# Expert stage of a two-layer trunk: permuted normed rows, picks dealt over the experts, modulation columns kept, gated rows dealt p-major

## What is computed

```python
def ec_moe(h, router_w, w1, w3, w2):
    cap = EC_CAPACITY_FACTOR * n // N_EXPERTS            # 2 * 256 // 16 = 32 tokens per expert
    affinity = jax.nn.softmax(h @ router_w, axis=-1)
    gate, idx = lax.top_k(jnp.swapaxes(affinity, 1, 2), cap)
    xg = jax.vmap(lambda hb, ib: hb[ib])(h, idx)
    hid = jax.nn.silu(jnp.einsum('becd,edf->becf', xg, w1)) * jnp.einsum('becd,edf->becf', xg, w3)
    out = jnp.einsum('becf,efd->becd', hid, w2) * gate[..., None]
    return jax.vmap(lambda ob, ib: jnp.zeros((n, d)).at[ib.reshape(-1)].add(ob.reshape(-1, d)))(out, idx)

def channel_sublayer(x, mod, ng, router_w, w1, w3, w2):
    h = modulate(rmsnorm(x, ng[2]), mod[3], mod[4])      # h * (1 + scale) + shift
    return x + mod[5] * rmsnorm(ec_moe(h, router_w, w1, w3, w2), ng[3])
```

## Time and profile before

| | us |
|---|---|
| three runs | 3607.09, 3611.14, 3621.99 |
| median | 3611.14 |
| profiled execution | 3622.84 |
| its span (first to last instruction) | 3620.3 |
| mean granted clock of TensorE | 0.887 of 2.4 GHz |
| layer 0: routing starts, first w1/w3 product | 1018.8, 1074.7 |
| layer 1: routing starts, first w1/w3 product | 2866.2, 2911.0 |

### The profile page before, as it was taken

One profiled execution on the slowest core, in us unless ns is written; L12 is line 12 of the kernel. 1 busy time (PEld: TensorE's weight loads), 2 busy tenths in 40 slices (PEclk: granted clock), 3 DMA queues, 4 the chain that ended last, 5 costly groups with the idle time before them and its releaser, 6 DMA issues. The chain is left out here.

```text
span 3620.3 us, 52864 instructions
## 1 busy us (share of the span) xinstructions
PE 2720.0 (75%) x23000; PEld 1436.8 (40%) x23000; DVE 901.3 (25%) x1911; ACT 521.6 (14%) x1070; POOL 301.9 (8%) x339
## 2 busy tenths in 40 slices
PE   5499966274958878788859477777777578888887
PEld 0144424242432424243324377666767323232322
DVE  1105025453031101010150154444445211010101
ACT  0100021321020000000120133322233100000001
POOL 0000000240010000000010222222222000000000
PEclk9799988696978999999979788888889799888999
DMA  9621100000248898989712200000000479999997
GB/s 384 251 71 70 70 0 1 0 1 29 76 166 360 346 409 340 402 347 405 299 50 71 102 12 12 12 12 12 12 12 3 184 290 372 401 387 410 371 416 304
DMA packets 107184, 676.36 MB, mean 187 GB/s; under 512 B 21240, under 2 KB 39456, under 8 KB 57424
## 3 DMA queue, kind: packets, MB, share of 16 engines
q1 hardware_dynamic: 105840, 672.44, 45.9%
q10 hardware_dynamic: 1120, 0.48, 0.0%
HBM read 666.37 MB, written 6.49 MB: 186 GB/s over the span
## 5 line engine op out<-in xcount | busy, mean ns | idle before, releaser
L1415 PE MATMUL bank<-moe_w,moe_xT 128*64 128x512 f32 (+3 forms) x3072 | 637.9, 570 | 79.1 <-DMA moe_w<-in_exp_w 76.5
L1442 PE MATMUL bank<-moe_w,moe_hidT 128*64 128x512 f32 (+1 forms) x1408 | 390.0, 711 | 116.9 <-DMA moe_w<-in_exp_w 105.5
L1415 PEld LDWEIGHTS bank<-moe_w,moe_xT 128*64 128x64 f32 (+1 forms) x3072 | 197.5, 126 | 520.7 <-issue 403.6
L1442 PEld LDWEIGHTS bank<-moe_w,moe_hidT 128*64 128x64 f32 (+1 forms) x1408 | 111.6, 144 | 363.6 <-issue 229.5
L1511 DVE TENSOR_TENSOR moe_silu<-bank,moe_silu 64x512 f32<-64x512 f32 (+3 forms) x96 | 56.6, 639 | 680.1 <-ACT moe_silu L1474 680.1
L1525 DVE COPY moe_rows<-bank 32x512 f32<-32x512 f32 x96 | 65.9, 686 | 551.5 <-PE bank L1442 550.6
L1474 ACT ACTIVATE moe_silu<-bank 64x512 f32<-64x512 f32 (+3 forms) x96 | 46.2, 545 | 1055.1 <-PE bank L1415 1055.1
L391 PE MATMUL bank<-w_slab,mixT 128*128 128x512 f32 x384 | 166.2, 593 | 1.9 <-PE bank L391 1.6
L2130 PE MATMUL bank<-x_inv_and_t,p_prod 64*64 64x64 f32 x2560 | 158.6, 219 | 4.7 <-issue 3.9
L1892 DVE TENSOR_TENSOR x_inv_and_t<-bank,x_inv_and_t 128x512 f32<-128x512 f32 (+1 forms) x160 | 102.2, 639 | 205.7 <-PE bank L2130 205.1
L388 PE MATMUL bank<-mixT,w_slab 128*128 128x512 f32 x320 | 141.6, 604 | 11.5 <-DMA w_slab<-in_ab_w_in 10.4
(11 more groups left out here) (460 smaller groups left out, 3219.9 us busy)
## 6 DMA issues: line engine op xcount, KB each, us to landing
moe_w<-in_exp_w SPq DMA_DIRECT2D x256, 1408.0 KB, 12.1
moe_w<-in_exp_w SPq DMA_DIRECT2D x64, 2048.0 KB, 19.2
ada_slab<-in_ada_w SPq DMA_DIRECT2D x32, 1536.0 KB, 12.8
moe_w<-in_exp_w SPq DMA_DIRECT2D x32, 1536.0 KB, 6.3
w_slab<-in_ab_w_in SPq DMA_DIRECT2D x11, 2048.0 KB, 7.6
wo_slab<-in_ab_w_out SPq DMA_DIRECT2D x16, 512.0 KB, 3.5
rw_slab<-in_rw_wk SPq DMA_DIRECT2D x4, 1024.0 KB, 7.4
rw_slab<-in_rw_wv SPq DMA_DIRECT2D x4, 1024.0 KB, 4.9
```

The costliest lines, as they stand in the source:

```text
L1415: mm = pe.matmul(g.ps[k][64 * m:64 * m + M, 0:hi - lo], xg[:, j, c, :], wa[:, sl, m, r, lo:hi], start=(c == 0), stop=(c == DC - 1))
L1442: mm = pe.matmul(g.ps[5 + m][64 * m:64 * m + M, :], hidt[:, c, :], wb[:, sl, c - lo, 512 * m:512 * m + 512], start=(c == 0), stop=(c == FC ...
```

## The change

- The modulation columns become a tile kept for the whole program (`g.modc`). They are loaded in `stage_out`, after `tail.load`, four small loads, and SyncE waits for them there; the loads and the wait in `stage_moe` are gone. L1229 and L1287 take their scale and shift from them.
- The normed rows are written permuted: chunk c holds columns c, c + 8, ... in a row, so that the picks' and the transposes' stationary operands are 128 words in a row. The router's weights are loaded to match.
- The picks of the next block are dealt: after w1/w3 of each expert of block i, quarter j of block i + 1, ahead of the wait for the gated product, all in bank 7. `moe_xT` gets two halves. VectorE's scaling (L1502) follows its gated product at each expert.
- The gated rows are dealt as they are written: SiLU and product write word q * 11 + c of the hidden row to place c * 128 + q, so the transposes read 128 words in a row. The three pieces are 506, 506 and 396 wide (before 512, 512, 384), to be multiples of 11.
- Small tiles of the routing move into space of larger ones; one memset moves to where the logits are awaited.

```diff
+    g.modc = keep("moe_mod_cols", [P, 2, 2, DC])
...
                 tail.load(sp)
+                for s in range(2):
+                    for k in range(2):
+                        sp.dma_start(g.modc[:, s, k, :], g.modp[layer, 1 - s:2 - s, (3 + k) * D:(4 + k) * D].rearrange("o (p c) -> p (o c)", c=DC)).then_inc(s_modc, 16)
+                sp.wait_ge(s_modc, 64)
...
-    SL = [(0, 512), (512, 1024), (1024, FF)]
+    SL = [(0, 46 * FC), (46 * FC, 92 * FC), (92 * FC, FF)]
...
-        xg = sb("moe_xT", [P, 4, DC, M])
+        xg = sb("moe_xT", [P, 2, 4, DC, M])
...
-                sp.dma_start(rw[:, :, 0:NE], a["router_w"][layer].rearrange("(c p) e -> p c e", p=P)).then_inc(s_rw, 16)
+                sp.dma_start(rw[:, :, 0:NE], a["router_w"][layer].rearrange("(p c) e -> p c e", c=DC)).then_inc(s_rw, 16)
...
-                for s in segs:
-                    for k in range(2):
-                        sp.dma_start(modc[:, s, k, :], g.modp[layer, 1 - s:2 - s, (3 + k) * D:(4 + k) * D].rearrange("o (p c) -> p (o c)", c=DC)).then_inc(s_modc, 16)
...
-                                       ACT.Identity, bias=g.cols[:, sh:sh + 1], scale=g.cols[:, col:col + 1]).then_inc(s_eva, 1)
+                                       ACT.Identity, bias=modc[:, t // 2, 0, dc:dc + 1], scale=modc[:, t // 2, 1, dc:dc + 1]).then_inc(s_eva, 1)
...
-                    dve.tensor_scalar(xn[:, t, :], g.x[:, t, :], norm[:, 2, t:t + 1], None, ALU.mult).then_inc(s_xn, 1)
...
+                    dve.tensor_scalar(xn[:, t, :].rearrange("p (c q) -> p q c", c=DC), g.x[:, t, :].rearrange("p (q c) -> p q c", c=DC),
+                                      norm[:, 2, t:t + 1], None, ALU.mult).then_inc(s_xn, 1)
...
+                dv.step(dve, dve.memset(lgt[:, :], 0.0))
...
-                dve.wait_ge(s_modc, 32 * ns)
...
-            PICK_BANK = (7, 0, 1, 2)
+            FIRST_BANK = (7, 0, 1, 2)
+            picked = lambda i, q: 2 * ns * (4 * i + q)
...
+                    if i:
+                        pe.wait_ge(s_x, picked(i, q))
...
-                                mm = pe.matmul(g.ps[PICK_BANK[q]][:, (k * ns + n) * P:(k * ns + n + 1) * P], xn[:, 2 * s + j, c::DC],
+                                mm = pe.matmul(g.ps[7 if i else FIRST_BANK[q]][:, (k * ns + n) * P:(k * ns + n + 1) * P], xn[:, 2 * s + j, c * P:(c + 1) * P],
...
+                    pe.wait_ge(s_x, picked(NB, 0))
...
-                    pe.wait_ge(s_x, 8 * ns * (i + 1))
+                    pe.wait_ge(s_x, picked(i + 1, 0))
...
-                    if j == 3 and i < NB - 1:
-                        if i == 0:
-                            pe.wait_ge(s_sto, min(3, len(PUT)))
-                        pick(i + 1, 0)
-                        pe.wait_ge(s_hid, e + 1)
-                        for q in range(1, 4):
-                            pick(i + 1, q)
+                    if i < NB - 1:
+                        if 0 < e <= len(PUT):
+                            pe.wait_ge(s_sto, e)
+                        pick(i + 1, j)
...
-                        mm = pe.transpose(g.ps[3 + c // 8][:, (c % 8) * M:(c % 8 + 1) * M], hid[:, c::FC], g.ident[0:M, 0:M])
+                        mm = pe.transpose(g.ps[3 + c // 8][:, (c % 8) * M:(c % 8 + 1) * M], hid[:, c * P:(c + 1) * P], g.ident[0:M, 0:M])
...
-                        if j:
-                            pe.wait_ge(s_sto, j)
+                        pe.wait_ge(s_x, picked(1, j + 1))
...
-                        act.activation(hid[:, lo:hi], g.ps[k][0:M, 0:hi - lo], ACT.Silu).then_inc(s_s, 1)
...
+                        act.activation(dealt(lo, hi), g.ps[k][0:M, 0:hi - lo].rearrange("m (q c) -> m q c", c=FC), ACT.Silu).then_inc(s_s, 1)
...
+                dealt = lambda lo, hi: hid[:, :].rearrange("m (c q) -> m q c", c=FC)[:, lo // FC:hi // FC, :]
...
-                        ins = dve.tensor_tensor(hid[:, lo:hi], g.ps[k][64:64 + M, 0:hi - lo], hid[:, lo:hi], ALU.mult)
+                        ins = dve.tensor_tensor(dealt(lo, hi), g.ps[k][64:64 + M, 0:hi - lo].rearrange("m (q c) -> m q c", c=FC), dealt(lo, hi), ALU.mult)
...
-                    if j == 3 and i < NB - 1:
-                        for q in range(4):
-                            rows_in(i + 1, q)
+                    if i < NB - 1:
+                        rows_in(i + 1, j)
```

More of the change, by code:

```diff
@@ L1091, in stage_out @@
         tail = Tail(g, ctx, layer, 2, t0)
-        s_w, s_used = [g.sem(f"wo_slab{i}") for i in range(RING)], g.sem("wo_used")
+        s_w, s_used, s_modc = [g.sem(f"wo_slab{i}") for i in range(RING)], g.sem("wo_used"), g.sem("moe_mod_cols")
         with nc.Block() as block:
@@ L1155, in stage_moe @@
         aff = sb("affinity", [P, 2, 48])
-        modc = sb("moe_mod_cols", [P, 2, 2, DC])
-        rw = sb("router_w", [P, DC, 32])
-        lgt = sb("logits_T", [P, P])
-        lg = sb("router_tmp", [P, 4, NE])
+        modc = g.modc
         st8 = sb("router_stat", [P, 4, 4])
-        atr = sb("affinity_rows", [48, SEG])
         mx = sb("top_values", [48, 8])
@@ L1188, in stage_moe @@
         s_wa, s_wb = [g.sem(f"moe_w13_{i}") for i in range(3)], [g.sem(f"moe_w2_{i}") for i in range(2)]
-        (s_rw, s_rwz, s_modc, s_sq, s_root, s_xn, s_tp, s_eva, s_evd, s_lg, s_lgc, s_lgt, s_max, s_e, s_aff, s_at, s_bd, s_bc, s_own) = (g.sem("route_" + n) for n in (
-            "weights", "weights_zeroed", "mod_cols", "squares", "root", "xn", "transposed", "out_scalar", "out_vector", "logits", "logits_kept", "logits_turned", "max", "exp", "affinity", "rows", "diag", "spread", "own"))
+        (s_rw, s_rwz, s_sq, s_root, s_xn, s_tp, s_eva, s_evd, s_lg, s_lgc, s_lgt, s_max, s_e, s_aff, s_at, s_bd, s_bc, s_own) = (g.sem("route_" + n) for n in (
+            "weights", "weights_zeroed", "squares", "root", "xn", "transposed", "out_scalar", "out_vector", "logits", "logits_kept", "logits_turned", "max", "exp", "affinity", "rows", "diag", "spread", "own"))
         with nc.Block() as block:
@@ L1227, in _ @@
                     for dc in range(4):
-                        col, sh = (mod_col(layer, 0 if t >= 2 else 1, 3 + k, dc) for k in (1, 0))
                         act.activation(hT[:, dc, t * P:(t + 1) * P], g.ps[2 * (n % 2)][:, dc * P:(dc + 1) * P],
-                                       ACT.Identity, bias=g.cols[:, sh:sh + 1], scale=g.cols[:, col:col + 1]).then_inc(s_eva, 1)
+                                       ACT.Identity, bias=modc[:, t // 2, 0, dc:dc + 1], scale=modc[:, t // 2, 1, dc:dc + 1]).then_inc(s_eva, 1)
                 act.wait_ge(s_max, 1)
@@ L1273, in _ @@
                 dv.do(dve.memset(aff[:, :, :], 0.0))
-                dv.do(dve.memset(lgt[:, :], 0.0))
                 def scaled(n):
@@ L1285, in out_half @@
                     for dc in range(4, DC):
-                        col, sh = (mod_col(layer, 0 if t >= 2 else 1, 3 + k, dc) for k in (1, 0))
                         dve.tensor_scalar(hT[:, dc, t * P:(t + 1) * P], g.ps[2 * (n % 2) + 1][:, (dc - 4) * P:(dc - 3) * P],
-                                          g.cols[:, col:col + 1], g.cols[:, sh:sh + 1], ALU.mult, ALU.add).then_inc(s_evd, 1)
+                                          modc[:, t // 2, 1, dc:dc + 1], modc[:, t // 2, 0, dc:dc + 1], ALU.mult, ALU.add).then_inc(s_evd, 1)
                 scaled(0)
```

14 lines of the change are left out of this document (9 added, 5 removed).

## The result

| | before | after |
|---|---|---|
| median, us | 3611.3 (4 runs, 3607.09 to 3621.99) | 3526.49 (4 runs, 3521.14 to 3533.57) |
| profiled execution, us | 3622.84 | 3522.6 |
| expert stage, layer 0 | 802.6 | 750.2 |
| RWKV stage (layer 1, its lines are unchanged) | 767.6 | 737.0 |
| expert stage, layer 1 | 751.4 | 733.7 |

The ratio is 0.9762, with an interval of 0.9733 to 0.9791: faster by 85 us. The stage rows run from the first to the last record of a stage's lines in the profiled executions; every other stage agrees within 0.6 us. So of the 100 us between the two profiled executions 70 lie in the expert stages and 31 in a stage that the change does not touch.

What follows compares the result with a forecast made beforehand. Weight loads by DMA were taken to bound the expert stages, running dry at boundary experts. Terms -20.6 - 7.5 - 50.3 + 26 + 4 = -48.4 us off the 3611.1 us median gave 3563 us, range 3528 to 3602.

Steps and rivals of the forecast that it cites:

- (a): Start of both expert stages: without the wait for modulation columns, masks start 8.4 and 12.2 us earlier, -20.6 us.
- (b): First block's picks in both layers: contiguous stationaries cut them from 15.4 to 9.9 and 7.7 to 5.7 us, -7.5 us.
- (c): Experts 3, 7, 11: with a quarter of the picks per expert, the boundary's whole excess over ordinary experts goes, -50.3 us.
- the normed rows' +4: Routing at the expert stages' start: permuted writes take 1.2 to 1.7 us per row instead of 0.75, +4 us (0 to 6.6).
- (d): Gap between w1/w3 and the transposes: strided writes lengthen it 1.2 us net at 21.5 experts, +26; normed rows add +4.
- rival of picks that keep the clock up: Layer 0, w2's first group: picks filling the gap save 2.2 us at 9 experts, -20 us, giving 3543 us; chance 0.10.
- the 43 to 44.5: Sign at ordinary experts: their windows should stay at 43 to 44.5 us each; leaving that would prove the forecast wrong.

Runs made afterwards that it cites:

- padded changed kernel: The changed kernel with 244 more already met wait instructions at the start of TensorE's list: 3572.23 us, ratio 0.9866 to the kernel before.
- padded kernel before: The kernel before with 12 more already met wait instructions at the start of TensorE's list: 3592.67 us, ratio 0.9914 to the kernel before.

## Why the forecast was off

Forecast -48.4, measured -85 (medians). The parts in turn, in sums of the two expert stages, means over the executions of each kernel, padded ones too: before 1555, kept columns -22, permuted rows -38, spread picks and dealt rows together -6 more, after 1489; with the gated rows in order 1472, which makes the spread -24 and the dealing +17. That is -66 in all. By the medians, the change without the RWKV stage is -58 (85 less 27, and 58 by the padded changed kernel too). The 8 us between are what single executions of one kernel differ by (1483.9 and 1491.5).

- **(a) Kept columns**, -20.6: measured -20.9 alone, by the named mechanism. Right. In layer 0 the masks start 2.1 us behind the spread products' start where 1.1 was taken, so the gain there is 7.4 for 8.4. The loads in the output projection cost nothing: from its first product to the start of the routing it is 126.7 us in both, and they land in 4.0 us in the median.
- **(b) First picks**, -7.5: 15.4 to 10.18 and 7.7 to 6.11 us, -6.8. Right; the normed rows, at 1.35 us each for 0.75, lie in the range given.
- **(c) Boundary**, -50.3: together with (b) and the normed rows' +4 the forecast was -54, and -61 was measured (1533.3 to 1472 in the expert stages). The sum is nearly right. How it arises was told too simply: contiguous stationaries alone take over half of it, either part leaves the other less to gain, and a part of what the spread picks gain in layer 0 lies at the ordinary experts.
- **(d) Dealt rows**, +26 and +4. The gap grew as worked out: 1.36 us for 1.35, though from other pieces, a first SiLU of 1.07 us (0.8 taken) and products 0.89 apart (0.95 taken). In means the product went from 0.639 to 0.948 us and SiLU from 0.545 to 0.986. The Trainium skill's page Vector Engine (DVE) Microarchitecture Reference, section Measured stream behaviour on trn2, gives 1.71 against 1.05 ns per column for a destination that hops every element. The product, which also reads one operand so, agrees in size: from its two widths, 1.87 ns per column (1024 and 818 ns for 506 and 396) against 1.03 before (689 and 557 ns for 512 and 384). The price of the gap was the mis-sized term: 17 to 20 us undone and 11.5 alone, for 26. Two things gave back, and both go with the clock. The transposes of layer 0 fell from 1.60 to 0.89 us, where 0.15 had been taken: strided loads take 1.41 to 1.42 us for 11 at either clock, contiguous ones 0.76 at full clock behind the picks and 1.25 at half clock behind an empty gap, so 0.15 would have been right without the picks. And in 7 to 9 of layer 0's 16 experts, for 4 before, w2's first group took 3.65 us. That is the rival of picks that keep the clock up, given 0.10. It is true at some experts of layer 0 and not in layer 1 (3 of 16, for 5 and 6 in the two executions of before). The same shows in the ordinary windows: 42.3 and 42.6 us each, below the 43 to 44.5 outside which the forecast called itself wrong.
- **What was not in the sum at all**: the RWKV stage, -27 by the medians of the padded kernel before, -31 by its ratio and by the traces. I costed added waits by who waits for them, and the code of an untouched stage at nothing. This step failed. Without it the kernel would be at 3526 + 27 = 3553, 10 us below the 3563 of the forecast and inside its range; (d), oversized by 6 to 9 us, and (c), short by 7, cover them. The Trainium skill's page Runtime: NRT & Kernel Launch, section Instruction fetch mechanics, says that lists are fetched in blocks of 16 KB, that crossing one is mostly hidden, and that a taken branch to outside the held window stalls the engine. The 16 KB packets agree, and so do the long stands at "issue" of 5.5 to 6.2 us, which come at the six jumps back and nowhere else in the stage. The second stand, of 2.1 to 2.8 us, is what 12 instructions remove. That it is the wait for the next block behind the jump is an argument: kernels with the long stage fetch 132 pieces in it and most others 126, six fewer for six jumps, but the one with 64 instructions more fetches 131 and has the short stage. If it is so, the crossing is not hidden there.

**Open.** Why the permuted rows took 5 us from RWKV (763.9 to 758.8), where a_hat,b_hat has its second stands as wherever the stage is long, isn't settled. Single executions of one kernel differ by up to 6 us in that stage, so it may be nothing. Nor is it settled what the half of the 30 us outside the second stands is, nor which places of the list lengthen it; beside that of before four were tried (7, 12, 76 and 256).

**What it comes to.** Gated rows written in order, with picks spread, stationaries contiguous and columns kept, take 3505 to 3509 us, 3% below the kernel before and 0.5% below the change.

## What to carry to other kernels

Before a change is credited, compare the stages that it doesn't touch: a loop on TensorE can gain or lose 4% when the list ahead of it grows by a dozen instructions, and a padded copy of the old kernel prices that. Two parts that remove the same loss are not to be added up; here stationaries without a stride were worth 38 us of the expert stages while the picks stood at the boundary, and nothing measurable once they stood in a covered gap. Useful work in a gap can pay twice, by its cover and by the clock of what follows. A stride moved from TensorE's reads to the writes of ScalarE and VectorE is paid by them on the path, 1.4 us for 0.7 saved in each expert.

## What was not expected of the hardware

- The place of TensorE's list: 12 already met waits at the start made an unchanged stage 31 us shorter (767.6 to 736.4), 256 made no difference, 76 were as good as 12.
- ScalarE's write with a step of 128 words: 1055 ns for 506 columns against 584 for 512 contiguous ones, worse than VectorE's 1024 against 689.
- Stationaries of 64 rows at a step of eleven words take 1.41 to 1.42 us for 11 loads at a clock of 1.00 and of 0.50 alike; contiguous ones take 0.76 at 1.00 and 1.25 at 0.50. So the step looked nearly free in the earlier trace rows, at half clock, beside the 128-row loads of the earlier trace rows.
- A short stand is dear twice: 48 picks took 5.62 us at a clock of 1.00 after a stand of 0.52, and 7.25 after one of 1.86, with the clock down to 0.71 in their first part. A stand of 2.50 us left it at 0.50 for the transposes behind it. w2's first group took 3.65 us at full clock and 5.0 to 6.6 where the clock had fallen.
- Each of the six jumps back in TensorE's list of the RWKV stage is followed by a stand of 5.5 to 6.2 us (once 7.15), in all 14 profiled executions.
